# Latent attention: the 64 key columns of a pair's two heads as one 128-wide stationary, and all heads' values from one chunk of 512 columns

## The chip, the cores and the metric

The kernel runs on one core of a Trainium2 chip. The metric is the device time of one execution in microseconds (us). TensorE is called PE here, VectorE DVE, ScalarE ACT, and SyncE SP. ACT and DVE copy and transform what PE leaves in PSUM, and SP issues nearly all weight transfers.

## The reference, cut to what matters

The program is four transformer layers on 512 tokens of width 1024, all in float32. The change touches the first layer alone, in its latent attention with 8 heads:

```python
c_q, c_kv, k_r = proj[..., :o1], proj[..., o1:o2], proj[..., o2:o3]      # 256, 128, 32 columns
qA = (_rmsnorm(c_q, g_q) @ w_uq).reshape(B_, S, MLA_HEADS, MLA_QK)       # 8 heads x 96
kv = (_rmsnorm(c_kv, g_kv) @ w_ukv).reshape(B_, S, MLA_HEADS, MLA_NOPE + MLA_V)   # 8 x (64 + 64)
k_nope, vA = kv[..., :MLA_NOPE], kv[..., MLA_NOPE:]
oA = _mla_causal_attention(concat(q_nope, q_rope), concat(k_nope, k_rope), vA)
```

So from the 128-wide latent of each token come 64 key columns and 64 value columns for each of the 8 heads. The 32 rotated key columns are the same for all heads. After causal softmax attention, the outputs of this and of a second, dilated attention (8 heads) go through one output projection, and a feed-forward block and three further layers follow.

## The kernel before

**Matmuls in three parts.** Every projection is done in fp32r with both operands split in a rounded high part and a low remainder. `mm3` (lines 316 to 321) issues three matmuls for each tile product: high by high (L319), and the two mixed ones (L320, L321). Tokens lie along the free axis, 512 of them, so that most matmuls are 128x128 stationary by 128x512 moving.

**The weight ring.** Weights come in chunks, in one order that is fixed for the whole program (`ORDER`). Chunk c lives in slot c mod 3. Each chunk is loaded by a DMA of SP, rounded by ACT (`round_weights`, L337) and split by DVE (`split_weights`, L345); only then may PE use it (semaphore `w_split`). The low part overwrites the raw data, so the DMA of chunk c + 3 waits until PE has used chunk c (`w_used`). Where ACT and DVE prepare a chunk is written out by hand: `round_weights(act, upto)` and `split_weights(dve, upto)` prepare everything not yet prepared up to chunk `upto`.

**The attention steps.** Heads are worked in pairs: four latent pairs (`mla`, p = 0 to 3), then four dilated pairs (`dil`). `att_pe`, `att_act` and `att_dve` each run one `step` for each pair m. In step m, PE computes the scores of pair m (`scores`, 8 blocks, in float32), the projections of pair m + 1 in `pieces`, placed between the other work by a tuple of shares, the transposes of the probabilities of pair m - 1 (`turn`, 20 transposes in four groups) and their product with the values (`pv`). ACT does the exponentials of pair m (`exps`), the copies of the transposes of pair m - 1 (`copies`), and the staging of the projected keys and values of pair m + 1 (`keys`, `values`). DVE rotates the queries (`rotate`), scales and masks the scores (`masks`) and divides by the row sums (`norm`).

**The latent pieces before.** A latent pair has two chunks: 512 elements per partition for the queries (`w_e_uq`) and 256 for keys and values (`w_e_ukv`), the latter in the order of the reference: key columns of head 0, value columns of head 0, key columns of head 1, value columns of head 1. `keys` uses each head's 128 columns (64 of keys, 64 of values) as one stationary and stores from each result only the upper 64 rows, so it takes two tiles of three matmuls with 512 columns. `values` takes the value columns as the moving operand: for each of four token tiles, three matmuls with 128 columns. `queries` takes two tiles of six matmuls. In step 0 there is no pair before, so there are no transposes.

**Preparing chunks before.** In step m, ACT rounds up to `early(pairs, R, m)` after its first four exponentials, and up to the last chunk of pair m + 2 at the end of the step. DVE does the same between its masks and `norm`, and after `norm`. `early` is the last chunk of pair m + 2, less one where that pair is latent: in step 0 that is the chunk with the queries of pair 2.

Of the kernel before, what the change touches and what calls it, by code (L numbers as in the profile page):

```python
# [123 lines left out]
def _build(nc, dram, ctx):  # L124
# [14 lines left out]
    st_mla = stage(mixed, 4, [(W["w_e_uq"], 512, 0, 1), (W["w_e_ukv"], 256, 0, 1)])  # L139
# [50 lines left out]
    def area(name, specs, start):  # L190

        at, out = start, []
        for n, shape, dt in specs:
# [17 lines left out]
    (e_cqh, e_cql, e_ckh, e_ckl, e_q0, e_q1, e_k0, e_k1, e_v0, e_v1, e_p, e_t0, e_causal, e_ropeq), _ = area("mla", [  # L211
# [4 lines left out]
         ("v0", (P, TB, P), F32), ("v1", (P, TB, P), F32),  # L216
# [719 lines left out]

    def heads_v(A, p, j):

        if A.kind == "dil":
            return A.v[:, p, j * P:(j + 1) * P]  # L940
        return A.v[p % len(A.v)][:, j, :]
# [27 lines left out]
    def last_chunk(pairs, R, m):  # L969

        if m >= len(pairs):
            return R.st.base + m - len(pairs)
        A, p = pairs[m]
        return A.st.base + (2 * p + 1 if A.kind == "mla" else p)
# [8 lines left out]
    def att_pe(pe, pairs, ready, R):  # L983
# [10 lines left out]
        def pieces(A, p):  # L994
# [15 lines left out]
            if A.kind == "dil":  # L1010
                c = A.st.base + p

                def one(which, k):
                    w_h, w_l = chunk_w(c, KD, 256)
                    if k == 0:
                        if which == 0:
                            pe.wait_ge(w_split, c + 1)
                            if p == 0:
                                wait_for(pe, a_mla.s["v_staged"], 4)
# [6 lines left out]
            c = A.st.base + 2 * p  # L1026
# [10 lines left out]
            def keys():  # L1037
                w_h, w_l = chunk_w(c + 1, 1, 256)
                pe.wait_ge(w_split, c + 2)
                for hh in range(2):  # L1040
                    wait_for(pe, s["q_staged"], 2 * p + hh + 1)
                    tile(A0 + hh, w_h, w_l, hh * P, (e_ckh, e_ckl), range(1), 1)\
                        .then_inc(keys_made, 1)

            def values(half):
                w_h, w_l = chunk_w(c + 1, 1, 256)
                vh = w_h[:, 0, :].rearrange("p (a b) -> p a b", a=2)[:, :, 64:P]
                vl = w_l[:, 0, :].rearrange("p (a b) -> p a b", a=2)[:, :, 64:P]
                if half == 0:
                    wait_for(pe, s["k_staged"], 2 * p + 1)  # L1050
                for t in (2 * half, 2 * half + 1):
                    last = mm3(pe, ps[:, A0, t * P:(t + 1) * P], e_ckh[:, 0, t * P:(t + 1) * P],
                               e_ckl[:, 0, t * P:(t + 1) * P], vh, vl, True, True)
                if half == 1:
                    last.then_inc(w_used, 1)
# [47 lines left out]
        def pv(A, p):  # L1103
# [4 lines left out]
            if A.kind == "mla":  # L1108
                wait_for(pe, s["v_staged"], p + 1)
# [75 lines left out]
    keys_made = sem("mla_keys_made")  # L1185

    def early(pairs, R, m):

        return last_chunk(pairs, R, m + 2) - (1 if m + 2 < len(pairs) and pairs[m + 2][0].kind == "mla" else 0)

    def att_act(act, pairs, R):
        def load_table(A, p):
# [3 lines left out]
            if A.kind == "dil" and p == 0:  # L1196
                act.wait_ge(w_used, st_mla.base + 8)
# [11 lines left out]
        def values(A, p):  # L1209
            act.wait_ge(w_used, A.st.base + 2 * p + 2)  # L1210
            act.activation(A.v[p % 3][:, :, :], ps[:, A0, :].rearrange("p (a b) -> p a b", a=TB),
                           ACT.Copy).then_inc(A.s["v_staged"].sem, 1)
# [39 lines left out]
        def step(m, cur, nx, prev, pp):  # L1252
            mla_next = nx and nx[0].kind == "mla"
            if nx:
# [1447 lines left out]
```

## Time and profile before

| | us |
|---|---|
| median of the 3 timed runs | 2314.56 |
| timed runs | 2314.78, 2309.9, 2314.56 |
| the profiled execution, its time | 2311.96 |
| its span | 2310.2 |
| mean granted clock | 0.998 |

The span goes from the first to the last instruction; 1.8 us of the profiled execution lie outside it. All times of instructions below are counted from the span's start. PE is the engine with the most busy time, 2285.1 us. Its matmuls are pipelined: a row's duration holds the time until the result is out, and the next matmul starts before that, so that the distance between two starts tells the pace. The four latent steps run from 61.05 us to 122 us or so; they are under 3% of the span.

### The profile page before, as it was taken

The page shows a single profiled execution, that of the slowest core. Times are in us where ns is not written, and L with a number is a line of the kernel's source. Part 1 is how long each engine was busy: PE and PEld are TensorE (multiplying, and loading weights), DVE is VectorE, ACT ScalarE, POOL GpSimd, SP SyncE. Part 2 cuts the span into 40 slices and gives each one's busy share as a digit, 9 for nine tenths or more (in the row PEclk, how much of TensorE's full clock was granted, in tenths as well). Part 3 has the DMA queues.
Part 4 walks back from the last instruction along what each step waited for, and adds up shares of the span by engine and source line. Part 5 has one row for each costly group of instructions (what it writes and reads, how often), then busy time and mean ns, then how long its engine had stood idle before and what let it go on. Part 6 is the DMA issues. An engine that isn't in the chain of part 4 may idle for free.

```text
span 2310.2 us, 26274 instructions
## 1 busy us (share of the span) xinstructions
PE 2285.1 (99%) x10812; PEld 1856.3 (80%) x10812; DVE 1124.0 (49%) x1732; ACT 891.3 (39%) x1414; POOL 0.2 (0%) x4
## 2 busy tenths in 40 slices
PE   9999999999999999999999999999999999999999
PEld 7777888888778888888888788888886667888887
DVE  5655443344575443445677654334444675432432
ACT  5654322223474322224434443223344785321321
POOL 0000000000000000000000000000000000000000
PEclk9999999999999999999999999999999999999999
DMA  4222222322222223222221132322332112223222
GB/s 143 80 83 73 91 89 101 104 93 88 92 92 73 93 91 105 104 80 99 100 65 55 55 110 91 109 92 91 104 104 73 55 55 73 92 91 108 93 91 92
DMA packets 36583, 206.52 MB, mean 89 GB/s; under 512 B 4192, under 2 KB 5088, under 8 KB 17136
## 3 DMA queue, kind: packets, MB, share of 16 engines
q1 hardware_dynamic: 34128, 199.43, 25.3%
q10 hardware_dynamic: 2336, 5.41, 0.7%
q8 instruction: 86, 1.41, 0.2%
q14 instruction: 33, 0.27, 0.0%
HBM read 202.73 MB, written 2.10 MB: 89 GB/s over the span
## 4 chain that ended last, share of the span: by engine, by line
PE 96%; DVE 2%; ACT 1%; issue 1%; DVEq 0%; ACTq 0%
PE ps L319 29%; PE ps L321 29%; PE ps L320 29%; PE ps L1075 2%; PE ps L1684 1%; PE ps L1130 1%; PE ps L2042 1%; PE ps L2061 1%; PE ps L1099 1%; PE ps L1125 1%; PE ps L2052 1%; PE ps L1091 0%; DVE low_w L345 0%; PE ps L1709 0%; PE ps L583 0%
## 5 line engine op out<-in xcount | busy, mean ns | idle before, releaser
L319 PE MATMUL ps<-xh,high_w 128*128 128x512 f32 x1592 | 631.8, 397 | 0.0
L321 PE MATMUL ps<-xh,low_w 128*128 128x512 f32 x1592 | 620.5, 390 | 0.0
L320 PE MATMUL ps<-xl,high_w 128*128 128x512 f32 x1592 | 620.0, 389 | 0.0
L345 DVE TENSOR_TENSOR low_w<-raw_w,high_w 128x2048 fp32r<-128x2048 f32 (+3 forms) x208 | 422.9, 2034 | 174.2 <-ACT high_w L337 173.8
L337 ACT ACTIVATE high_w<-raw_w 128x2048 fp32r<-128x2048 f32 (+3 forms) x208 | 353.3, 1700 | 287.9 <-PE ps L321 281.4
L319 PEld LDWEIGHTS ps<-xh,high_w 128*128 128x128 f32 x1592 | 299.0, 188 | 65.1 <-issue 5.5
L321 PEld LDWEIGHTS ps<-xh,low_w 128*128 128x128 f32 x1592 | 298.8, 188 | 62.9
L320 PEld LDWEIGHTS ps<-xl,high_w 128*128 128x128 f32 x1592 | 299.2, 188 | 61.1 <-issue 1.4
L319 PE MATMUL ps<-ffn_hidh,high_w 128*128 128x512 f32 x864 | 336.1, 389 | 0.0
L320 PE MATMUL ps<-ffn_hidl,high_w 128*128 128x512 f32 x864 | 336.1, 389 | 0.0
L321 PE MATMUL ps<-ffn_hidh,low_w 128*128 128x512 f32 x864 | 336.1, 389 | 0.0
L713 DVE TENSOR_TENSOR h<-h,ps 128x512 f32<-128x512 f32 (+1 forms) x80 | 63.6, 794 | 327.7 <-PE ps L321 327.7
L320 PEld LDWEIGHTS ps<-ffn_hidl,high_w 128*128 128x128 f32 x864 | 162.2, 188 | 33.8
L319 PEld LDWEIGHTS ps<-ffn_hidh,high_w 128*128 128x128 f32 x864 | 162.2, 188 | 33.6
L321 PEld LDWEIGHTS ps<-ffn_hidh,low_w 128*128 128x128 f32 x864 | 162.2, 188 | 33.5
L761 ACT ACTIVATE squares_sq<-squares_sq 128x512 f32<-128x512 f32 x44 | 27.8, 632 | 334.7 <-DVE squares_sq L785 334.7
L785 DVE TENSOR_TENSOR squares_sq<-ps,rstd 128x512 f32<-128x512 f32 x44 | 30.4, 692 | 216.9 <-PE ps L321 205.9
L769 ACT ACTIVATE squares_sq<-squares_sq 128x512 f32<-128x512 f32 x64 | 39.3, 632 | 208.6 <-DVE squares_sq L801 208.6
L485 ACT ACTIVATE xh<-h,gains 128x512 fp32r<-128x512 f32 x56 | 38.7, 719 | 181.4 <-DVE h L713 178.6
L801 DVE SCALAR_TENSOR_TENSOR squares_sq<-ps,rstd 128x512 f32<-128x512 f32 x64 | 41.2, 686 | 126.4 <-PE ps L321 115.4
L319 PE MATMUL ps<-mix_oh,high_w 128*128 128x512 f32 x192 | 78.4, 408 | 0.0
L319 PE MATMUL ps<-high_w,xh 128*128 128x256 f32 (+1 forms) x224 | 76.7, 342 | 0.3 <-DVE low_w L345 0.3
(280 smaller groups left out, 2452.3 us busy)
## 6 DMA issues: line engine op xcount, KB each, us to landing
raw_w<-in_w_f_gu SPq DMA_DIRECT2D x44, 1024.0 KB, 4.9
raw_w<-in_w_m_up SPq DMA_DIRECT2D x32, 1024.0 KB, 4.8
raw_w<-in_w_m_dn SPq DMA_DIRECT2D x32, 1024.0 KB, 4.9
raw_w<-in_w_f_dn SPq DMA_DIRECT2D x32, 704.0 KB, 4.0
raw_w<-in_w_b_qk SPq DMA_DIRECT2D x8, 1024.0 KB, 4.9
raw_w<-in_w_e_qk SPq DMA_DIRECT2D x4, 1024.0 KB, 5.2
raw_w<-in_w_e_out SPq DMA_DIRECT2D x4, 1024.0 KB, 5.6
raw_w<-in_w_o_q SPq DMA_DIRECT2D x8, 512.0 KB, 3.6
```

The lines of the kernel that those rows point to most:

```text
L319: pe.matmul(out, sh, mh, start=start, stop=False)
L320: pe.matmul(out, sh, ml, start=False, stop=False)
L321: return pe.matmul(out, sl, mh, start=False, stop=stop)
L337: act.activation(wh[slot][:, 0:elems], raw[slot][:, 0:elems], ACT.Copy).then_inc(w_rounded, 1)
L345: dve.tensor_tensor(wl[slot][:, 0:elems], raw[slot][:, 0:elems], wh[slot][:, 0:elems].bitcast(F32), ALU.subtract).then_inc(w_split, 1)
L485: act.activation(hi[:, t, :], h[:, t, :], ACT.Copy, scale=weight(t)).then_inc(F.s["rounded"].sem, 1)
L713: dve.tensor_tensor(to, to, ps[:, 2 * par:2 * par + R.nt, :], ALU.add).then_inc(R.added.sem, 1)
L761: act.activation(sq[:, par, :], sq[:, par, :], ACT.Silu).then_inc(s["acted"].sem, 1)
L769: act.activation(sq[:, 2 + j, :], sq[:, j, :], ACT.Square).then_inc(s["acted"].sem, 1)
L785: dve.tensor_tensor(sq[:, par, :], ps[:, 2 * par, :], rstd[:, :], ALU.mult)\
L801: dve.scalar_tensor_tensor(out=sq[:, j, :], in0=ps[:, 2 * par + j, :], scalar=0.0, in1=rstd[:, :], op0=ALU.max, op1=ALU.mult)\
L1075: pe.matmul(score_block(A, n), heads_q(A, st, hh, i), heads_k(A, st, hh, i), start=True, stop=True).then_inc(s["scored"].sem, 1)
```

## The change

The weights for keys and values are packed in another way. Each pair now has a chunk `w_e_uk` of 128 elements per partition with the 64 key columns of both heads side by side, and one chunk `w_e_uv` of 512 elements holds the value columns of all eight heads. The latent stage has nine chunks instead of eight: queries 0, keys 0, queries 1, keys 1, all values, queries 2, keys 2, queries 3, keys 3. `keys` is one tile of three matmuls for a pair, and ACT takes its upper 64 rows for one head and its lower 64 rows for the other. `values(t)` is done once, in step 0, for one token tile t of 128 tokens and all heads: three matmuls with 512 columns, into four PSUM banks, which ACT copies one at a time into `e_v` and `xf`. `pv` of every latent pair reads from there.

```diff
-    st_mla = stage(mixed, 4, [(W["w_e_uq"], 512, 0, 1), (W["w_e_ukv"], 256, 0, 1)])
+    st_mla = stage(Stage, [entry for p in range(4) for entry in
+                           [(W["w_e_uq"], 512, p), (W["w_e_uk"], P, p)] + [(W["w_e_uv"], 512, 0)] * (p == 1)])
...
+    def mla_chunk(p):
+
+        return st_mla.base + 2 * p + (1 if p > 1 else 0)
+
+    st_mla_v = st_mla.base + 4
+    MLA_V_BANK = (O_BANK, T_BANK, T_BANK + 1, A1)
...
-                wait_past(pe, s["v_staged"], p)
+                if p == 2:
+                    wait_for(pe, s["v_staged"], 4)
...
             def keys():
-                w_h, w_l = chunk_w(c + 1, 1, 256)
+                w_h, w_l = chunk_w(c + 1, 1, P)
                 pe.wait_ge(w_split, c + 2)
-                for hh in range(2):
-                    wait_for(pe, s["q_staged"], 2 * p + hh + 1)
-                    tile(A0 + hh, w_h, w_l, hh * P, (e_ckh, e_ckl), range(1), 1)\
-                        .then_inc(keys_made, 1)
-
-            def values(half):
...
-            return [queries, keys, lambda: values(0), lambda: values(1)], (1, 1, 1, 0, 1)
+                wait_for(pe, s["q_staged"], 2 * p + 1)
+                tile(A0, w_h, w_l, 0, (e_ckh, e_ckl), range(1), 1).then_inc(w_used, 1)
+
+            def values(t):
+                w_h, w_l = chunk_w(st_mla_v, 1, 512)
+                if t == 0:
+                    pe.wait_ge(w_split, st_mla_v + 1)
...
+                last = mm3(pe, ps[:, MLA_V_BANK[t], :], e_ckh[:, 0, t * P:(t + 1) * P],
+                           e_ckl[:, 0, t * P:(t + 1) * P], w_h[:, 0, :], w_l[:, 0, :], True, True)
+                last.then_inc(w_used if t == 3 else latent_values_made, 1)
+            if p == 1:
+                return [queries, keys] + [lambda t=t: values(t) for t in range(TB)], (1, 2, 1, 1, 1)
+            return [queries, keys], (1, 1, 0, 0, 0)
...
+                if A.kind == "mla" and p == 1:
+                    wait_for(pe, s["v_staged"], 2)
+            if A.kind == "mla" and p == 1 and ns[0] == 4:
+                wait_for(pe, s["v_staged"], 3)
...
     def early(pairs, R, m):
 
+        if m == 0 and pairs[0][0].kind == "mla":
+            return st_mla_v
...
         def keys(A, p):
+            act.wait_ge(w_used, mla_chunk(p) + 2)
             for hh in range(2):
-                act.wait_ge(keys_made, 2 * p + hh + 1)
-                act.activation(A.k[p % 2][0:64, hh, :], ps[0:64, A0 + hh, :], ACT.Copy)\
+                act.activation(A.k[p % 2][0:64, hh, :], ps[64 * hh:64 * hh + 64, A0, :], ACT.Copy)\
...
             if mla_next:
                 keys(*nx)
+            if first_mla:
+                values(cur[0], (0,))
...
             exps(*cur, range(6, 7))
+            if first_mla:
+                values(cur[0], (1,))
...
-            if mla_next:
-                values(*nx)
+            if first_mla:
+                values(cur[0], (2, 3))
...
+            if m == 0 and cur[0].kind == "mla":
+                split_weights(dve, st_mla_v)
             if cur[0].kind != "swa":
                 masks(*cur, range(4, 8))
```

How this moves instructions is read from the instruction order of the two programs. On DVE, at the end of step 0 before the change (low_w_59 is the low part of the queries' chunk of pair 2, low_w_57 that of its keys and values, the RECIPROCAL and the eight TENSOR_SCALAR after it are `norm`; the rows with squares_sq begin step 1):

```order
L1336 ISA small 128x1
L345 TENSOR_TENSOR low_w_59<-raw_w_56,high_w_53 128x512
L1352 RECIPROCAL small<-small 128x8
L1356 TENSOR_SCALAR mla_p<-mla_p,small 128x128
L1356 TENSOR_SCALAR mla_p<-mla_p,small 128x256
L1356 TENSOR_SCALAR mla_p<-mla_p,small 128x384
...
L345 TENSOR_TENSOR low_w_57<-raw_w_54,high_w_51 128x256
L1336 ISA squares_sq,small<-ps,mla_causal 128x128
```

And the same place on DVE with the change (low_w_57 is now the low part of the queries' chunk of pair 2, low_w_58 that of its keys):

```order
L1364 ISA small 128x1
L1380 RECIPROCAL small<-small 128x8
L1384 TENSOR_SCALAR mla_p<-mla_p,small 128x128
L1384 TENSOR_SCALAR mla_p<-mla_p,small 128x256
L1384 TENSOR_SCALAR mla_p<-mla_p,small 128x384
...
L346 TENSOR_TENSOR low_w_57<-raw_w_54,high_w_51 128x512
L346 TENSOR_TENSOR low_w_58<-raw_w_55,high_w_52 128x128
L1364 ISA squares_sq,small<-ps,mla_causal 128x128
```

The split of the chunk with the queries of pair 2 has moved from ahead of `norm` to behind it. In its old place ahead of the masks, not shown, stands the split of the chunk with all values.

On ACT, in step 0 before the change, from the fifth exponential on (L1220 with mla_p is an exponential, L1206 stages keys, L1211 values, L337 rounds a chunk):

```order
L337 ACTIVATE high_w_53<-raw_w_56 128x512
L1220 ACTIVATE mla_p,small<-mla_p,small 128x384 x2
L1206 ACTIVATE mla_k_70<-ps 64x512 x2
L1220 ACTIVATE mla_p,small<-mla_p,small 128x512 x2
L1211 ACTIVATE mla_v_72<-ps 128x512
L337 ACTIVATE high_w_51<-raw_w_54 128x256
```

And the same stretch of ACT with the change (L1244 is an exponential, L1226 stages keys, L1235 values, L338 rounds a chunk):

```order
L338 ACTIVATE high_w_53<-raw_w_56 128x512
L1244 ACTIVATE mla_p,small<-mla_p,small 128x384 x2
L1226 ACTIVATE mla_k_70<-ps 64x512 x2
L1235 ACTIVATE mla_v<-ps 128x512
L1244 ACTIVATE mla_p,small<-mla_p,small 128x512
L1235 ACTIVATE mla_v<-ps 128x512
L1244 ACTIVATE mla_p,small<-mla_p,small 128x512
L1235 ACTIVATE xf<-ps 128x512 x2
L338 ACTIVATE high_w_51<-raw_w_54 128x512
L338 ACTIVATE high_w_52<-raw_w_55 128x128
```

Two copies of values now stand ahead of the last exponential. The rounding of the queries' chunk of pair 2, once the first row of this stretch, now stands behind the four copies.

## Rows read from the trace of the kernel before

**Rows 1.** The page: span and busy time of PE.

```profile
span 2310.2 us, 26274 instructions
PE 2285.1 (99%) x10812; PEld 1856.3 (80%) x10812; DVE 1124.0 (49%) x1732; ACT 891.3 (39%) x1414; POOL 0.2 (0%) x4
```

**Rows 2.** Instructions of the tile mla_ckh: durations min/median/max, first and last start.

```profile
L319 PE MATMUL ps<-high_w,mla_ckh x16: 222/274/327, 59.8 to 100.4; 128*128 128x128 f32 x16
```

**Rows 3.** Timeline 58.2 to 62.3 us: start, duration, engine, line, [idle before <-releaser].

```profile
58.25 0.39 PE L320 MATMUL ps<-mla_ckl,high_w 128*128 128x512 f32 x1
58.47 0.39 PE L321 MATMUL ps<-mla_ckh,low_w 128*128 128x512 f32 x1
58.90 0.59 ACT L1206 ACTIVATE mla_k<-ps 64x512 f32<-64x512 f32 x1 [0.97 <-PE ps L321]
...
59.76 0.22 PE L319 MATMUL ps<-high_w,mla_ckh 128*128 128x128 f32 x1
...
60.46 0.92 ACT L337 ACTIVATE high_w<-raw_w 128x512 fp32r<-128x512 f32 x2
...
61.05 1.52 PE L1075 MATMUL ps<-mla_k,mla_q 128*128 128x128 f32 x8
61.11 1.03 DVE L345 TENSOR_TENSOR low_w<-raw_w,high_w 128x512 fp32r<-128x512 f32 x2 [2.20 <-ACT high_w L337]
...
62.23 0.58 PE L319 MATMUL ps<-mla_cqh,high_w 128*128 128x512 f32 x1
```

**Rows 4.** Timeline 65.3 to 74.4 us, the rest of step 0 and after.

```profile
65.36 0.69 DVE L1307 TENSOR_TENSOR mla_q<-ps,mla_ropeq 128x512 f32<-128x512 f32 x1 [0.67 <-PE ps L321]
...
68.48 0.69 DVE L1336 CUSTOM_DVE_ANT_0 mla_p<-ps,mla_causal 128x512 f32<-128x512 f32 x1 [0.16 <-PE ps L1075]
...
69.06 1.27 ACT L1206 ACTIVATE mla_k<-ps 64x512 f32<-64x512 f32 x2 [0.99 <-PE ps L321]
...
70.94 0.71 ACT L1220 ACTIVATE mla_p<-mla_p,small 128x512 f32<-128x512 f32 x1
...
71.10 1.52 PE L1075 MATMUL ps<-mla_k,mla_q 128*128 128x128 f32 x8
...
71.64 0.58 ACT L1211 ACTIVATE mla_v<-ps 128x512 f32<-128x512 f32 x1
71.77 0.20 DVE L1352 RECIPROCAL small<-small 128x8 f32<-128x8 f32 x1 [1.99 <-ACT mla_p L1220]
...
72.32 0.54 PE L319 MATMUL ps<-mla_cqh,high_w 128*128 128x512 f32 x1
...
74.38 0.42 DVE L345 TENSOR_TENSOR low_w<-raw_w,high_w 128x256 fp32r<-128x256 f32 x1
```

**Rows 5.** Timeline of step 1: first transposes, staging of keys, first pv matmul.

```profile
78.20 0.49 PE L1099 MATMUL ps<-ident,mla_p 128*128 128x128 f32 x3
...
80.21 1.06 ACT L1206 ACTIVATE mla_k<-ps 64x512 f32<-64x512 f32 x2
...
84.87 0.64 PE L1130 MATMUL ps<-mla_t,mla_v 128*64 128x512 f32 x1 [0.16 <-ACT mlat_t L1243]
```

**Rows 6.** Windows: ACT in step 1; columns are us, ACT busy, PEclk, DMA.

```profile
78.51:84.87 6.36, 6.36 (x19) 1.00 0.01 3
```

**Rows 7.** Waits of PE over the whole span: total, times, longest.

```profile
PE ps L1684 <- DVE gla_ks L1865: 4.3, 4, 1.8
PE ps L2052 <- DVE small L2296: 2.5, 1, 2.5
PE ps L2022 <- ACT squares_sq L2133: 2.4, 1, 2.4
```

**Rows 8.** Windows of PE just after those three longest waits.

```profile
1299.80:1303.90 4.10, 3.95 (x14) 0.59 0.00 0
1779.60:1783.00 3.40, 3.40 (x13) 1.00 0.53 222
1908.10:1911.50 3.40, 3.40 (x13) 0.50 0.00 0
```

More of the change, by code:

```diff
@@ L973, in last_chunk @@
         A, p = pairs[m]
-        return A.st.base + (2 * p + 1 if A.kind == "mla" else p)
+        return mla_chunk(p) + 1 if A.kind == "mla" else A.st.base + p
     def att_steps(pairs, step, tail):
@@ L1024, in pieces @@
                 return [lambda a=a, k=k: one(a, k) for a in range(2) for k in range(KD)], (4, 3, 3, 3, 3)
-            c = A.st.base + 2 * p
+            c = mla_chunk(p)
             def queries():
@@ L1037, in keys @@
             def keys():
-                w_h, w_l = chunk_w(c + 1, 1, 256)
+                w_h, w_l = chunk_w(c + 1, 1, P)
                 pe.wait_ge(w_split, c + 2)
-                for hh in range(2):
-                    wait_for(pe, s["q_staged"], 2 * p + hh + 1)
-                    tile(A0 + hh, w_h, w_l, hh * P, (e_ckh, e_ckl), range(1), 1)\
-                        .then_inc(keys_made, 1)
-            def values(half):
[L1046 to L1055, printed above, removed]
-            return [queries, keys, lambda: values(0), lambda: values(1)], (1, 1, 1, 0, 1)
+                wait_for(pe, s["q_staged"], 2 * p + 1)
[4 more added lines that the diff above has]
+                    pe.wait_ge(w_split, st_mla_v + 1)
+                elif t == 3:
+                    wait_for(pe, s["q_staged"], 4)
+                else:
+                    wait_for(pe, s["masked"], 3 + t)
+                last = mm3(pe, ps[:, MLA_V_BANK[t], :], e_ckh[:, 0, t * P:(t + 1) * P],
[4 more added lines that the diff above has]
+            return [queries, keys], (1, 1, 0, 0, 0)
         def scores(A, p, ns):
@@ L1108, in pv @@
             if A.kind == "mla":
-                wait_for(pe, s["v_staged"], p + 1)
+                wait_for(pe, s["v_staged"], 4)
             if A.kind == "swa" and p == 0:
@@ L1196, in load_table @@
             if A.kind == "dil" and p == 0:
-                act.wait_ge(w_used, st_mla.base + 8)
+                act.wait_ge(w_used, st_mla.base + 9)
             wait_past(act, A.s["masked"], 8 * (p - 1))
@@ L1203, in keys, with values @@
         def keys(A, p):
+            act.wait_ge(w_used, mla_chunk(p) + 2)
             for hh in range(2):
-                act.wait_ge(keys_made, 2 * p + hh + 1)
-                act.activation(A.k[p % 2][0:64, hh, :], ps[0:64, A0 + hh, :], ACT.Copy)\
+                act.activation(A.k[p % 2][0:64, hh, :], ps[64 * hh:64 * hh + 64, A0, :], ACT.Copy)\
                    .then_inc(A.s["k_staged"].sem, 1)
[L1209 to L1212, printed above, removed]
+        def values(A, ts):
+            for t in ts:
+                if t == 3:
+                    act.wait_ge(w_used, st_mla_v + 1)
+                else:
+                    act.wait_ge(latent_values_made, t + 1)
+                act.activation(latent_values(t), ps[:, MLA_V_BANK[t], :], ACT.Copy)\
+                   .then_inc(A.s["v_staged"].sem, 1)
         def exps(A, p, ns):
@@ L1253, in step @@
             mla_next = nx and nx[0].kind == "mla"
+            first_mla = m == 0 and cur[0].kind == "mla"
             if nx:
@@ L1292, in att_act @@
             round_weights(act, last_chunk(pairs, R, 1))
-            values(*pairs[0])
         att_steps(pairs, step, tail)
@@ L1303, in rotate @@
                 if hh:
-                    dve.wait_ge(w_used, A.st.base + 2 * p + 1)
+                    dve.wait_ge(w_used, mla_chunk(p) + 1)
                 else:
@@ L2621, in lay_out @@
     arrays["w_e_uq"] = panels(a["e_w_uq"][0], [np.concatenate(cols[2 * i:2 * i + 2]) for i in range(4)])
-    arrays["w_e_ukv"] = panels(a["e_w_ukv"][0], [r(256 * i, 256 * i + 256) for i in range(4)])
+    heads = r(1024).reshape(8, 2, 64)
+    arrays["w_e_uk"] = panels(a["e_w_ukv"][0], [heads[2 * i:2 * i + 2, 0].reshape(-1) for i in range(4)])
+    arrays["w_e_uv"] = panels(a["e_w_ukv"][0], [heads[:, 1].reshape(-1)])
     q0, k0, v0 = 416, 416 + 512, 416 + 1024
```

14 lines of the change are left out of this document (9 added, 5 removed).

## The prediction

> **What bounds the kernel now.** I read the page first. PE is busy for 2285.1 of 2310.2 us [rows 1], so work that is taken from PE is gained where nothing else ends last, and only there. The change touches less than 3% of the span, the latent steps, so I then read their timeline.
>
> The reader is to see three stretches there. In the *opening* (58 to 61 us), PE goes from the key tiles through the value matmuls to the scores. The matmuls with 512 columns start 0.22 to 0.23 us apart [rows 3]. I take 0.227. The twelve with 128 columns take from 59.76 to 61.05, 0.108 each [rows 3], where a quarter of the columns would be 0.057.
>
> In *step 0* there is no other pair to turn, and PE runs nearly without a wait to the scores of step 1 at 71.10 and the queries of pair 2 at 72.32 [rows 4]. DVE does `norm` just then: the reciprocal at 71.77, the next split at 74.38 [rows 4]. The queries of pair 2 didn't have to wait for it, because their chunk was split ahead of `norm`.
>
> In *step 1* (and step 2 repeats it) the engine that sets the end is another one. The first transposes start at 78.20, `pv` at 84.87 after a wait for ACT's last copy [rows 5], and from 78.51 to 84.87 ACT is busy for 6.36 of 6.36 us [rows 6]: copies, two exponentials, the staging of keys, copies, and so on, each in the order written. PE's keys, transposes and value matmuls lie inside this stretch and are not what it waits for.
>
> **The change part by part.** *Counted on PE alone.* Keys lose 4 x 3 = 12 matmuls of 512 columns, 12 x 0.227 = 2.7 us. The 48 value matmuls of 128 columns (16 on each of three lines [rows 2], 4 x 1.3 = 5.2 us) become 12 of 512. The trace doesn't show these with this stationary; the bounds are 12 x 0.108 = 1.3, if the added columns were free, and 12 x 0.39 = 4.7, if none overlapped the next [rows 3]. I take 12 x 0.227 = 2.7 us, the pace of the rows with as many columns. So values gain 2.5 us. By count the change is worth 5.2 us. The Trainium skill ("TensorE: Matmul & The Clock Gate", section on the back-to-back issue gap) gives about 81 ns for a matmul with 128 columns and 131 ns for one with 512 in a stream that reloads weights; by it keys would give 12 x 0.131 = 1.6 and values 3.9 - 1.6 = 2.3, together 3.9 us. The rows above don't agree with either figure, and they decide.
>
> *The opening.* The keys' only tile starts when the first of two did and its last matmul is the one at 58.47; ACT took its result at 58.90 [rows 3]. Now ACT copies both heads from it. Two such copies in a row take 1.06 us where one takes 0.59 [rows 3, 5], so a row ends with about 0.1 that the next instruction overlaps, and ACT is free after 0.96. So the scores can start at 58.90 + 1.06 + 0.06 = 60.02 instead of 61.05 [rows 3]. Of 2.0 us of PE work removed here (0.7 keys, 1.3 values) 1.03 is gained, the rest becomes a wait of PE for ACT. The rounding of the next chunk moves from 60.46 to 59.86, its split from 61.11 to 60.5, done by 61.2 [rows 3]; the queries of pair 1 start at 61.25, not 62.23. From here step 0 runs 0.97 ahead.
>
> That the second copy reads PSUM partitions 64 to 127 and writes 0 to 63 is shown nowhere. Below it costs what the other one does, 0.59 [rows 3]; above I put twice that, 0.6 more in each step. I take nothing.
>
> *Step 0.* The second rotation starts at 64.39 instead of 65.36 and takes 0.69 [rows 4]. Behind it now stands the split of the values' chunk, 0.69 for 512 elements like this, and pushes the four masks back by up to 0.6, so the last one starts no later than its 68.48 of before [rows 4], while ACT stages keys: that is cover enough. PE finishes the keys 0.97 + 0.69 earlier than before; ACT took the first tile at 69.06 and takes the only tile at 68.09. Then ACT's order decides: keys 0.96, values(0) 0.58, an exponential 0.71, values(1) 0.58, and the last exponential starts at 70.9, as before at 70.94 [rows 4]. All that was gained is gone on ACT by now. PE's twelve value matmuls end their issue at 70.6 (72.6 by the upper bound, still ahead of the stall below); the scores of step 1 wait for values(1) and start at 70.95, 0.15 ahead of before.
>
> *Where it stalls.* Behind the last exponential ACT does values(2), values(3) (1.2) and rounds the queries' chunk of pair 2 (0.62), until 73.4. DVE had split that chunk ahead of `norm`. Now `norm` comes first. It begins at 71.73, 0.83 behind the last exponential's start as before (70.94 to 71.77), and takes 2.61 (71.77 to 74.38) [rows 4], until 74.35. Then the split takes 0.69, until 75.05. PE, in order, stands at the queries of pair 2: ready at 72.15, held to 75.05. Before, they began at 72.32 with a first matmul that took 0.15 more than usual, so 72.4. **Loss: 2.65 us.** PE's queue behind it holds the scores 4 to 7 and the transposes, and ACT's chain of step 1 starts with the transposes.
>
> The wait for `v_staged` 4 in `queries` (ACT at 72.7) and the other new waits end before that. The DMAs are no later: each of the nine chunks is issued when its slot is free, all of it before the stall, and the large chunks behind them come one slot earlier than before.
>
> *Steps 1 and 2.* PE loses 0.7 of keys and 1.3 of values in each, 4.0 us, inside the stretch of 6.67 us from the first transposes to `pv` [rows 5], all of it ACT's [rows 6]. ACT's list in that stretch is the same with the change (its copy of values came behind it). Gain: nothing. Without this cover it would be 4.0. Step 3 and all behind it stream on PE and keep the shift.
>
> *The clock.* The three longest waits of PE in the span are 1.8, 2.5 and 2.4 us [rows 7]. After the first, the granted clock is 0.59 over 4.1 us; after the second, 0.50 over 3.4 us, the lower of the two levels; after the third it stays at 1.00 [rows 8]. The new wait is about 2.5 us without any matmul in flight. At half clock for 3.4 us with PE's work on the path the loss is at most 1.7; I take 1.6. The chance is 2 in 3 by count; I take 6 in 10, since there are only three cases. The Trainium skill ("TensorE: Matmul & The Clock Gate", section on the clock gate) says that the lower level is the default and activity releases it, which these rows bear out.
>
> *The sum.* 2.65 + 1.6 = 4.25. Against the profiled execution's own 2311.96 (span 2310.2 and 1.8 around it) this gives 2316.2; against the median of the three runs, 2314.56, which is 2.6 higher, 2318.8. The four executions scatter over 4.9 us, so I take the middle of the two bases, 2313.3, and predict **2317.5 us**, 0.18% more than before. What a measurement of this kernel can tell from no change is 0.2%, 4.6 us.
>
> **The rivals.**
>
> *The stall alone.* The clock stays. For it speaks the wait of 2.4 us after which it did [rows 8]. 2313.3 + 2.65 = 2316.0.
>
> *PE is the bound in steps 1 and 2 after all.* The page says 99% PE [rows 1], and if ACT had slack of its own that is only filled because PE delays it, the 4.0 us would come back. Against it: ACT's 6.36 of 6.36 us. 2313.3 + 2.65 - 4.0 = 2311.9.
>
> *The other side: no stall.* If `norm` and the split before PE's queries took no longer than to 72.4, the count would hold: 2313.3 - 5.2 = 2308.1. It decides at the point where the split ends by 72.4, and the order puts 2.6 us of `norm` ahead of it that can't start before the last exponential. Only if PE waited elsewhere anyway would it not show.
>
> *A dearer one, slower by more than 0.2%.* The staging of head 1's keys across partitions costs 0.6 more each time: once in the opening, once in step 0 ahead of the last exponential, once each in the chains of steps 1 and 2. In the opening and in step 0 it moves the same stall, so it counts once there; 3 x 0.6 = 1.8 on top of 4.25: 2313.3 + 6.0 = 2319.3. With 0.13 more for each it crosses the bound of 4.6. Against it: a copy of 64 partitions takes 0.59 and one of 128 partitions 0.58 [rows 3, 4], so partitions don't matter for its time.
>
> **How the numbers follow.** Stall with the fall of the clock 0.42, stall alone 0.28, dearer 0.12, PE the bound 0.10, no stall 0.08. The range leaves out no stall and the upper half of the dearest: 2311.5 (PE the bound, less 0.4) to 2320.5 (dearest with the higher base). Faster by over 0.2% is no stall, 0.08. Slower by over 0.2% is the dearer case and, since 4.25 lies just under 4.6, somewhat under half of the first, 0.12 + 0.19 = 0.31. The rest, 0.61, is within 0.2%.
>
> **What would show it right or wrong.** After: the first matmul with mla_cqh of pair 2 starts about 2.9 us behind the scores of step 1, and its releaser is DVE's low_w, behind the eight TENSOR_SCALAR. ACT's last exponential of step 0 stands behind a copy of values and starts at 70.7 to 71.1. From the first transposes of step 1 to its `pv` 6.7 us pass as before, with PE less busy. From the scores of step 1 to those of step 2 it takes 2.8 us longer, or 4.4 with a PEclk of 0.5 in it; from there to the end the shift is constant. It would be wrong if ACT's stretch in steps 1 and 2 got shorter, if PE's wait in front of the queries ended at 73 us, or if the shift at step 3's start were not the shift at the end.

## The result and the profile after

The changed kernel takes 2321.13 us (median of 5 runs, 2317.91 to 2322.5), the kernel before 2313.95 us (median of 5, 2309.9 to 2314.78). The ratio is 1.0034, with a 95% interval of 1.0023 to 1.0045: slower by 7.2 us by the medians and by 7.9 us by the ratio, where 2317.5 and a difference of 4.25 were forecast. The time lies outside the range of 2311.5 to 2320.5.

The profiled execution took 2321.05 us. Its page, where the kernel before had 2285.1 us of PE in 2310.2 [rows 1]:

```profile
span 2319.3 us, 26183 instructions
PE 2283.9 (98%) x10764; PEld 1852.1 (80%) x10764; DVE 1124.6 (48%) x1733; ACT 891.7 (38%) x1415; POOL 0.2 (0%) x4
```

PE has 48 matmuls less and is busy for 1.2 us less, and the span is 9.1 us longer. The opening and step 0 on the timeline, which answers to [rows 3] and [rows 4] (start, duration, engine, line, [idle before <-releaser]; L1226 stages keys, L1235 values, L1244 is an exponential, L1384 is the last part of `norm`, L346 a split):

```profile
58.82 1.21 ACT L1226 ACTIVATE mla_k<-ps 64x512 f32<-64x512 f32 x2 [0.98 <-PE ps L322]
60.13 1.55 PE L1093 MATMUL ps<-mla_k,mla_q 128*128 128x128 f32 x8 [1.34 <-issue]
...
71.08 0.72 ACT L1244 ACTIVATE mla_p<-mla_p,small 128x512 f32<-128x512 f32 x1
...
71.44 1.55 PE L1093 MATMUL ps<-mla_k,mla_q 128*128 128x128 f32 x8 [0.59 <-ACT mla_v L1235]
...
71.92 0.20 DVE L1380 RECIPROCAL small<-small 128x8 f32<-128x8 f32 x1 [3.64 <-ACT mla_p L1244]
72.16 2.46 DVE L1384 TENSOR_SCALAR mla_p<-mla_p,small 128x128 f32<-128x128 f32 x8
...
74.53 0.89 DVE L346 TENSOR_TENSOR low_w<-raw_w,high_w 128x512 fp32r<-128x512 f32 x2
75.27 0.50 PE L320 MATMUL ps<-mla_cqh,high_w 128*128 128x512 f32 x1 [2.28 <-DVE low_w L346]
```

The scores of step 0 start at 60.13 instead of 61.05, after 1.34 us of idle time for which the row names no releaser; they start 0.10 behind the end of the two key copies (58.82 + 1.21). The last exponential starts at 71.08, `norm` makes way for the next split at 74.53, and the queries of pair 2 start at 75.27 behind DVE's split, after a wait of 2.28 us. Steps 1 and 2, which answer to [rows 5]:

```profile
81.14 0.49 PE L1117 MATMUL ps<-ident,mla_p 128*128 128x128 f32 x3
...
83.15 1.20 ACT L1226 ACTIVATE mla_k<-ps 64x512 f32<-64x512 f32 x2
84.37 0.98 ACT L1267 ACTIVATE mla_t<-ps 128x384 f32<-128x384 f32 x2
85.00 0.30 PE L1117 MATMUL ps<-ident,mla_p 128*128 128x128 f32 x1 [1.91 <-ACT mla_t L1267]
...
88.11 1.11 PE L1148 MATMUL ps<-mla_t,mla_v 128*64 128x512 f32 x1 [0.69 <-ACT mlat_t L1267]
...
92.57 2.20 PE L1093 MATMUL ps<-mla_k,mla_q 128*128 128x128 f32 x8
...
94.42 0.58 PE L320 MATMUL ps<-mla_cqh,high_w 128*128 128x512 f32 x1
...
104.24 0.30 PE L1117 MATMUL ps<-ident,mlap_p 128*128 128x128 f32 x1 [1.91 <-ACT mla_t L1267]
...
107.35 0.95 PE L1148 MATMUL ps<-mla_t,mla_v 128*64 128x512 f32 x1 [0.80 <-ACT mlat_t L1267]
...
111.34 1.58 PE L1093 MATMUL ps<-mla_k,mla_q 128*128 128x128 f32 x8
```

And PE in three windows of the same execution (us, PE busy, PEclk, DMA): its queries right behind the wait of 2.28 us, then the two stretches in which the granted clock was low.

```profile
75.27:78.14 2.87, 2.87 (x12) 1.00 0.00 0
87.07:93.89 6.82, 6.13 (x24) 0.50 0.01 2
107.55:110.96 3.41, 3.41 (x12) 0.50 0.47 154
```

The reader is to see that the first transposes come 2.94 us later than before (81.14 for 78.20 [rows 5]), and that this is not the end of it. A `pv` matmul with 512 columns, which took 0.64 [rows 5], takes 1.11. The clock did not fall behind the wait of 2.28 us, where it stayed at 1.00. It fell to 0.50, its level of 1.2 GHz, late in step 1 for 6.8 us and again late in step 2 for 3.4 us. What PE waited for between 60 and 116 us (total, times, longest):

```profile
PE ps L1117 <- ACT mla_t L1267: 4.2, 4, 1.9
PE ps L320 <- DVE low_w L346: 2.3, 1, 2.3
PE ps L1148 <- ACT mlat_t L1267: 1.5, 2, 0.8
PE ps L1093 <- issue: 1.3, 1, 1.3
PE ps L1117 <- ACT mlat_t L1267: 0.9, 2, 0.5
PE ps L1093 <- ACT mla_v L1235: 0.6, 1, 0.6
```

Together 10.8 us. The same view of the kernel before, in the same stretch, adds up to 1.6 us: its second key tile and half of its value matmuls stood in the place of the wait of 1.9 us of each step, the other half ahead of `pv`.

### The profile page after: what moved, and what is told of

Its sections match the earlier page's. It is cut to its first block, busy times and chain, and to the rows that moved or that the text cites. A ratio compares the mean times of both kernels' runs of the same rounds, so it can differ in the third digit from the quotient of the medians.

```text
span 2319.3 us, 26183 instructions
## 1 busy us (share of the span) xinstructions
PE 2283.9 (98%) x10764; PEld 1852.1 (80%) x10764; DVE 1124.6 (48%) x1733; ACT 891.7 (38%) x1415; POOL 0.2 (0%) x4
## 4 chain that ended last, share of the span: by engine, by line
PE 95%; DVE 2%; ACT 2%; issue 1%; ACTq 0%; DVEq 0%
PE ps L320 29%; PE ps L322 28%; PE ps L321 28%; PE ps L1093 2%; PE ps L1714 1%; PE ps L1148 1%; PE ps L2072 1%; PE ps L2091 1%; PE ps L1117 1%; PE ps L1143 1%; PE ps L2082 1%; PE ps L1109 0%; DVE low_w L346 0%; PE ps L1739 0%; PE ps L584 0%
## 5 line engine op out<-in xcount | busy, mean ns | idle before, releaser
L346 DVE TENSOR_TENSOR low_w<-raw_w,high_w 128x2048 fp32r<-128x2048 f32 (+4 forms) x209 | 423.0, 2026 | 173.4 <-ACT high_w L338 173.0
L338 ACT ACTIVATE high_w<-raw_w 128x2048 fp32r<-128x2048 f32 (+4 forms) x209 | 353.4, 1693 | 288.2 <-PE ps L322 281.5
```

The source lines that it names most:

```text
L338: act.activation(wh[slot][:, 0:elems], raw[slot][:, 0:elems], ACT.Copy).then_inc(w_rounded, 1)
L346: dve.tensor_tensor(wl[slot][:, 0:elems], raw[slot][:, 0:elems], wh[slot][:, 0:elems].bitcast(F32), ALU.subtract).then_inc(w_split, 1)
```

## The experiments

The experiments were timed in three groups of four, each in turns with the kernel before; the changed kernel's row is the result above. The first group is fill, early, keysonly and novals; the second is fill_a1, early_fill_a1, keys_a1 and keys_dve; the third, on another chip than these two, is fill_all, early_fill_all, early_dve and before_dve. The ratio is to the kernel before in the same group. "Clock" is the mean, over the timed runs, of the granted TensorE clock that each run lists. "Step 3" is when its scores start in the profiled execution, in us, a stretch that ends ahead of everything the kernels have in common. One execution of `early` took 8171.46 us and is left out, so its ratio rests on four.

Two things limit what the table can tell. The profiled execution is one of the timed ones and often an extreme one: in fill_all and early_dve it is the fastest of 11, in novals, early_fill_all, keys_dve and before_dve the slowest of 11. And the mean clock also holds the falls behind step 3, where the code is the same. In the profiled executions the lower clock there adds up to 10.2 us in the kernel before and in the changed one, but to 13.6 in novals, 17.0 in keys_dve, 20.4 in early_fill_all and 23.8 in before_dve, which has no fall at all between 60 and 116 us. A difference of 0.001 in the mean clock of some ten executions therefore doesn't say by itself where the clock fell.

Three accounts of the loss stand against each other in the expectations. Clock theory: the removed matmuls kept PE busy beside ACT's list, and without them the clock falls. Stall theory: the late split and the dearer key copies are all of it. PE-bound theory: PE's work is what ends these steps, so less of it is faster.

| kernel | ratio (95% interval) | clock | step 3 |
|---|---|---|---|
| before | 1 | 0.9980, 0.9981, 0.9975 in the three groups | 103.3 |
| changed | 1.0034 (1.0023 to 1.0045) | 0.9956 | 111.3 |
| early | 1.0038 (1.0025 to 1.0052) | 0.9942 | 109.6 |
| fill | 1.0030 (1.0018 to 1.0041) | 0.9963 | 107.3 |
| fill_a1 | 1.0025 (1.0016 to 1.0033) | 0.9967 | 110.1 |
| fill_all | 1.0016 (1.0007 to 1.0025) | 0.9969 | 106.7 |
| early_fill_a1 | 1.0019 (1.0010 to 1.0028) | 0.9963 | 110.1 |
| early_fill_all | 1.0012 (1.0003 to 1.0021) | 0.9969 | 105.3 |
| novals | 1.0013 (1.0004 to 1.0022) | 0.9965 | 106.5 |
| keysonly | 1.0032 (1.0022 to 1.0042) | 0.9952 | 110.6 |
| keys_a1 | 1.0025 (1.0015 to 1.0035) | 0.9949 | 107.1 |
| keys_dve | 0.9987 (0.9978 to 0.9995) | 0.9979 | 101.6 |
| before_dve | 1.0008 (0.9999 to 1.0017) | 0.9969 | 105.7 |
| early_dve | 1.0006 (0.9997 to 1.0015) | 0.9963 | 103.8 |

**Less work alone (novals).** The edit of the kernel before leaves out 22 of the 24 small value matmuls of pairs 2 and 3, so that their values are not computed, and adds no wait:

```diff
+                if p > 1:
+                    if half == 1:
+                        pe.matmul(ps[:, A0, 3 * P:TOK], e_ckh[:, 0, 3 * P:TOK], vh, start=True, stop=True)\
+                            .then_inc(w_used, 1)
+                    return
```

> The kernel before, which leaves out 11 of the 12 value matmuls of each of pairs 2 and 3 (the values of these pairs are wrong; ACT still copies the bank). 22 matmuls, 2.4 us of PE work less, nothing added, no wait added. Clock theory: PE now waits about 1.7 us in each of steps 1 and 2 and the clock falls behind it, so the kernel with less work gets slower by 2 to 4.5 us, 1.0009 to 1.0020, PEclk 0.5 for 3.4 to 6.8 us between 80 and 112 us. Stall theory: no change, 1.0000. PE-bound theory: 2.4 us faster, 0.9990.

It is slower by 0.13%, 3.0 us, as the clock theory had forecast (1.0009 to 1.0020). PE in step 1, where the matmuls are gone, and the window that follows:

```profile
81.99 0.30 PE L1104 MATMUL ps<-ident,mla_p 128*128 128x128 f32 x1 [0.93 <-ACT mla_t L1248]
...
85.08 1.11 PE L1135 MATMUL ps<-mla_t,mla_v 128*64 128x512 f32 x1 [0.72 <-ACT mlat_t L1248]
...
84.30:91.10 6.80, 6.08 (x23) 0.50 0.45 157
```

Waits of 0.93 and 0.72 us stand where the value matmuls were, none as long as those that the prediction looked at. The clock falls at 84.31, behind the first of them and two of 0.18 and 0.46 us, and stays at 0.50 for 6.8 us; the wait of 0.72 lies in the fall. From the first transposes to `pv` it takes 6.67 us (78.41 to 85.08), as before: the work taken away was worth nothing. Step 2 then starts at 89.5 for 87.17 of before and step 3 at 106.5 for 103.3, 3.1 us later, of which 0.2 was there ahead of step 1. This execution is the slowest of the 11 and lost as much again behind step 3. The timed runs say the same another way: at a mean clock of 0.996 novals averages 2317.4 us (7 executions) and the kernel before 2317.0 (3 in the same group), so what separates them is how often the clock is low. Shown: idle time of PE in ACT's stretch costs by the clock, without any other part of the change.

**The work put back (fill, fill_a1, fill_all).** The changed kernel, with matmuls whose results nobody reads. fill and fill_a1 put back the 12 small value matmuls of each of pairs 2 and 3, fill_all the second key tile too. This is fill_all's edit. fill_a1 lacks the first three lines and waits for the second query tile instead of the first key copy; fill writes to the keys' bank `A0` and waits for both key copies:

```diff
+                if p > 1:
+                    wait_for(pe, s["q_staged"], 2 * p + 2)
+                    tile(A1, w_h, w_l, 0, (e_ckh, e_ckl), range(1), 1)
...
+            def filler(half):
+                w_h, w_l = chunk_w(c + 1, 1, P)
+                if half == 0:
+                    wait_for(pe, s["k_staged"], 2 * p + 1)
+                for t in (2 * half, 2 * half + 1):
+                    last = mm3(pe, ps[:, A1, t * P:(t + 1) * P], e_ckh[:, 0, t * P:(t + 1) * P],
+                               e_ckl[:, 0, t * P:(t + 1) * P], w_h[:, 0, :], w_l[:, 0, :], True, True)
...
+            if p > 1:
+                return [queries, keys, lambda: filler(0), lambda: filler(1)], (1, 1, 1, 0, 1)
```

> The changed kernel, and for pairs 2 and 3 PE again does the 12 value matmuls of 128 columns of each pair where they stood before, with the keys' chunk as moving operand; nobody reads the result. Clock theory (PE's value matmuls kept PE busy beside ACT's chain, and without them the granted clock falls): with more work the kernel gets faster by about 4.5 us against the changed one, PEclk 1.00 from 80 to 112 us, step 2 starts 2.7 us earlier and step 3 4.4 us earlier than in the changed kernel; ratio to the kernel before about 1.0015. Stall theory (the wait for the low part of pair 2's queries and the dearer key copies are all of it): no change against the changed kernel, ratio 1.0034. PE-bound theory: up to 2.6 us slower than the changed kernel, 1.0045.

> As fill, but the unread value matmuls go to the bank of the second query tile and so need not wait for the key copies, which left a wait of 1.3 us in fill. Clock theory: no wait of PE over 1 us and no PEclk under 1.00 between 80 and 115 us in most executions; mean granted clock of the timed runs 0.997 to 0.998 (changed kernel 0.995 to 0.996); ratio to before 1.0014 to 1.0020, what is left being the wait of 2.3 us at 75 us, 0.7 for the start of step 1 and 0.25 to 0.3 for the key copies in each of steps 1 and 2. Stall theory: 1.0034 as the changed kernel.

> The changed kernel, with all of PE's work of before back in steps 1 and 2 and unread: for pairs 2 and 3 a second key tile of three matmuls with 512 columns and the 12 value matmuls, in the bank of the second query tile, the values behind the first key copy as before. fill and fill_a1 left out the key tile and kept waits of 1.3 us. Clock theory: mean granted clock of the timed runs back at 0.998 (changed kernel 0.9956), ratio 1.0012 to 1.0018, which is the stall of step 1 (2.9 us) and the dearer key copies (0.3 in each of steps 1 and 2) alone. If PE's waits in steps 1 and 2 are not what brings the clock down: mean clock stays at 0.996, ratio 1.0025 to 1.0034.

fill_all has all of PE's work of before in steps 1 and 2, and more work makes it faster than the changed kernel. Its PE from 80 to 112 us, and its waits in front of the transposes there:

```profile
80.00:112.00 32.00, 29.70 (x163) 1.00 0.34 116
PE ps L1132 <- ACT mla_t L1286: 1.1, 4, 0.3
PE ps L1132 <- ACT mlat_t L1286: 0.9, 2, 0.5
```

The clock is 1.00 throughout, no wait is over 0.5 us, the longest of the kernel before there, and step 3 starts at 106.7 instead of 111.3, with the wait of 2.3 us at 75 us still there. The ratio is 1.0016, as was forecast for the stall and the copies alone. The mean clock was forecast to come back to 0.998; it is 0.9969, against 0.9975 of its group. The interval (1.0007 to 1.0025) only just overlaps that of the changed kernel (1.0023 to 1.0045), and the two were not timed in the same group, so the gain in the timed runs is likely rather than beyond doubt. At equal mean clock fill_all is 2.3 to 3.1 us slower than the kernel before of its group, and the changed kernel 2.2 to 3.0, so what separates these two is the clock.

fill and fill_a1 lie above the forecast of the clock theory (1.0015, and 1.0014 to 1.0020) with 1.0030 and 1.0025. Waits of 1.3 us remained in their steps 1 and 2. In fill's profiled execution the clock held all the same, in fill_a1's it fell at 102.7 us for 6.8 us. Each ratio is within the other's interval and within that of the changed kernel. fill's interval (1.0018 to 1.0041) leaves out the 1.0015 but not the 1.0034 of the stall theory, and fill_a1's (1.0016 to 1.0033) reaches from the forecast to just short of 1.0034. So the timed runs leave open whether the half fills give anything.

**The stall alone taken away (early).** ACT rounds the queries' chunk of pair 2 ahead of values(0), DVE splits it ahead of `norm`:

```diff
+                round_weights(act, st_mla_v + 1)
                 values(cur[0], (0,))
...
+            if m == 0 and cur[0].kind == "mla":
+                split_weights(dve, st_mla_v + 1)
```

> The changed kernel, with the queries' chunk of pair 2 rounded by ACT ahead of values(0) and split by DVE ahead of norm. Stall theory: the wait of 2.3 us at 75.3 is gone, transposes of step 1 start 2.3 to 2.9 us earlier, ratio to the kernel before about 1.0022 to 1.0024. Clock theory: the same 2.3 to 2.9 us come back, but the waits of 1.9 us in steps 1 and 2 and the fall of the clock behind them remain, 4.5 us of them, so the kernel stays slower than before, 1.0022; if the wait at 75.3 was what made the clock fall at 87, the clock now stays and the ratio is about 1.0010.

The wait at 75.3 is gone, and the first transposes of step 1 start at 79.5 instead of 81.14. That is less than expected, since ACT's list of step 0 is now longer by the rounding and the scores of step 1 start at 72.1. The clock falls at 85.1 us for 6.8 us and at 105.6 for 3.4 us as in the changed kernel, without a wait over 2 us anywhere near. Step 3 starts 1.7 us earlier. By the timed runs nothing is gained: the ratio is 1.0038 where both theories had about 1.0022, it overlaps the changed kernel's almost wholly, and the mean clock, of four executions, is the lowest of all. So the wait for the split is not what brings the clock down.

**Both (early_fill_a1, early_fill_all).** Their edits are those above together.

> fill_a1 and early together. If the late split and the missing fill are all of the loss beside the key copies: ratio 1.0005 to 1.0012 (early had the transposes of step 1 at 79.5, 1.3 us behind the kernel before, and each key staging costs 0.3). If the fall of the clock has another cause than PE's waits in steps 1 and 2: 1.0025 or more.

> fill_all and early together: the queries' chunk of pair 2 is prepared ahead of norm too. Clock theory: mean clock 0.998, ratio 1.0004 to 1.0010. Otherwise 1.0019 or more, as early_fill_a1.

early_fill_all is at 1.0012, a little above the 1.0004 to 1.0010 expected, with step 3 at 105.3 and no fall of the clock between 60 and 116 us in its profile. What remains of 2.0 us there is the start of step 1, 1.1 us late since PE waits for ACT's copies of the values of all pairs, 0.2 more up to the first transposes, and 0.3 in each chain for the keys. early_fill_a1, with waits of 1.3 us left, had the lower clock for 3.4 us from 85.9 and for 6.8 us from 103.0 in its profile. Its 1.0019 lies between the two forecasts, 1.0005 to 1.0012 and 1.0025 or more, and decides nothing.

**The keys' part alone (keysonly, keys_a1, keys_dve).** The kernel before with the chunk packed as both heads' keys, then both heads' values, and one key tile:

```diff
-                for hh in range(2):
-                    wait_for(pe, s["q_staged"], 2 * p + hh + 1)
-                    tile(A0 + hh, w_h, w_l, hh * P, (e_ckh, e_ckl), range(1), 1)\
+                wait_for(pe, s["q_staged"], 2 * p + 1)
+                tile(A0, w_h, w_l, 0, (e_ckh, e_ckl), range(1), 1).then_inc(keys_made, 1)
```

In keysonly the values use the same bank as the keys, and wait for both copies. In keys_a1 they use the bank of the second query tile. keys_dve is keys_a1 with the second head's copy on DVE:

```diff
+        def second_keys(A, p):
+            dve.wait_ge(keys_made, p + 1)
+            dve.tensor_copy(A.k[p % 2][0:64, 1, :], ps[64:P, A0, :]).then_inc(A.s["k_staged"].sem, 1)
...
             split_weights(dve, early(pairs, R, m))
+            if nx_kind == "mla":
+                second_keys(*nx)
```

> The kernel before with the keys' part of the change alone: the pair's chunk holds both heads' key columns, then both heads' value columns, one key tile for a pair, values for each pair as before. Clock theory: the value matmuls still fill PE beside ACT's chain; only the second key copy costs 0.25 us more in steps 1 and 2, the opening gains some tenths (PE waits for both copies before the values), ratio 0.9998 to 1.0006. PE-count theory: 12 matmuls of 0.227 less, 2.7 us faster, 0.9988. If the keys' part alone lets the clock fall, 1.0015 or more, with PEclk under 1.00 between 80 and 112 us.

> As keysonly, but the values go to the bank of the second query tile, so that they need not wait for both key copies (keysonly had a wait of 1.3 us in front of the values of every pair). Clock theory: the waits and the fall of the clock at 61, 85 and 106 us are gone; ratio 0.9995 to 1.0006, mean clock 0.998. If one key tile for two heads is dear by itself, 1.003 as keysonly.

> As keys_a1, and DVE takes the second head's key copy, behind its masks, where it waits for ACT anyway. ACT's stretch from the first transposes to pv gets shorter by one key copy, 0.5 to 0.6 us in steps 1 and 2 each, the opening by about 0.7 us: ratio 0.9985 to 0.9995 if the clock holds. If ACT's order isn't what ends steps 1 and 2: as keys_a1. A shorter stretch leaves PE less to wait for, so the clock should hold better than in keys_a1.

The first two miss the forecast of the clock theory (0.9998 to 1.0006, 0.9995 to 1.0006) and come out at the dear end that was named beside it. I had overlooked that one tile for both heads makes the values wait for two copies where they waited for one: four waits of 1.3 us in keysonly, and the clock falls at 61, 85 and 106 us. In keys_a1, with fewer matmuls and the longer copies, waits of 1.3 us stand in front of the third group of transposes, and the clock falls at 99.9 us. Both have 12 large matmuls less than before and are slower.

keys_dve is faster than the kernel before, and than the changed one. Its waits of PE on ACT in the same stretch, and the copy on DVE beside ACT's:

```profile
PE ps L1096 <- ACT mla_t L1238: 1.4, 4, 0.5
PE ps L1096 <- ACT mlat_t L1238: 0.9, 2, 0.5
...
79.09 0.69 DVE L1307 COPY mla_k<-ps 64x512 f32<-64x512 f32 x1
...
79.46 0.58 ACT L1202 ACTIVATE mla_k<-ps 64x512 f32<-64x512 f32 x1
```

From the first transposes to `pv` it takes 6.18 us (77.45 to 83.63) instead of the 6.67 of before, and step 3 starts 1.7 us earlier. No fall of the clock lies between 60 and 116 us. The profiled execution as a whole is the slowest of the 11, 2314.2 us, with 17.0 us at the lower clock behind step 3; the median is 2309.86.

**Where keys_dve's gain comes from (before_dve, early_dve).** The same copy on DVE in the kernel before with its two key tiles, and in `early`, that is in the whole change:

> The kernel before, with DVE taking the second head's key copy alone (two key tiles for a pair, old packing). It tells how much of keys_dve's 0.9987 is the key tile. If ACT's list is what ends steps 1 and 2, most of the gain is here: 0.9988 to 0.9996. If the one key tile is what pays: 1.0000.

> The whole change with the early preparation of the queries' chunk of pair 2 and with DVE taking the second head's key copy, no filler. ACT's stretch in steps 1 and 2 gets 0.6 us shorter each, ACT's list of step 0 too, so the stall at 72 to 75 us nearly goes: by the shifts alone 0.9985 to 0.9995. Clock theory: PE waits more than in keys_dve (no value matmuls in steps 1 and 2), the clock falls as in the changed kernel (mean 0.996) and gives back 3 to 5 us: 1.0000 to 1.0012, slower than keys_dve (0.9987). If only ACT's list counts: 0.9985 or less.

before_dve has the short chain in step 1 (80.57 to 86.76), but not in step 2, where it takes 7.16 us (96.24 to 103.40) and PE waits 1.21 us for DVE's copy. Its step 0 starts 1.6 us late: DVE's copy has to wait for the second key tile, and the values in the first bank wait for both copies, so step 1 starts at 73.5 for 71.1. It is not faster, 1.0008, where 0.9988 to 0.9996 or 1.0000 was expected. So the copy on DVE pays with one key tile and a bank of its own for the values, not by itself. early_dve has no small value matmuls and no filler; its step 2 starts at 86.8, 0.4 earlier than before. Then the clock falls at 99.5 us, and it ends at 1.0006 with a mean clock of 0.9963, against 0.9979 of keys_dve, which keeps the small value matmuls in steps 1 and 2.

## Why the prediction was wrong

**The opening** was right: scores from 60.13, forecast 60.02. The queries of pair 1 started at 61.33, forecast 61.25.

**Step 0 and the stall** were right: the last exponential at 71.08 (forecast 70.9), `norm` until 74.5 (74.35), queries of pair 2 from 75.27 (75.05). Only the scores of step 1 came later than forecast, 71.44 for 70.95, without effect on the stall. The shift at the first transposes is 2.94 us (2.65). That ACT's list gives back all that the opening gained, and that moving one split behind `norm` costs more than that, came out as read.

**The keys' staging across partitions**, taken at nothing with an upper bound of 0.6, costs 0.3: the pair takes 1.20 instead of 1.06 and the next instruction starts 1.22 behind instead of 0.96 (83.15 to 84.37; the kernel before had 80.21 [rows 5] and 81.17). Each copy by itself still takes 0.58 to 0.59; what is lost is the overlap of the second with its neighbours, which start 0.60 and 0.62 us apart instead of 0.48. From the first transposes to `pv` it is 6.97 instead of 6.67, twice, 0.6 us in all. The dearer rival's extra cost was real, at half its price.

**The failing step** is "Steps 1 and 2 ... Gain: nothing." Nothing was gained, as said, but the step priced the removed work at nothing, and it was worth something. PE's second key tile and value matmuls were not on ACT's path; they filled PE's time beside it. Without them PE waits 1.9 us in front of the third group of transposes in each of the two steps, and 0.7 to 0.8 ahead of `pv`. The clock fell to half at 87.07, just ahead of the wait for `pv`, and at 107.55, 0.2 us into `pv`, so PE did `pv` at the lower clock, and in step 1 the next scores too; both are on the path. From `pv` to the scores of the next step it took 4.46 us in step 1 and 3.99 in step 2, where `pv` had taken 2.30 each time (84.87 [rows 5] to 87.17, 101.03 to 103.33), and the four scores behind step 1 took 1.85 instead of 1.23: 2.16 + 0.62 + 1.69 = 4.5 us. With the stall's 2.94 and the copies' 0.6 this makes 8.0, the shift of step 3 (111.34 for 103.33).

**The term for the clock** had the right size for one fall of 3.4 us (1.6, measured 1.69 in step 2) and the wrong place and number: 1.6 in all, where the two falls cost 4.5. It was tied to the one wait that looked long, chosen by the three waits in [rows 7]. The clock did not fall behind it, fell twice elsewhere, and the experiments show it to go with the shorter, repeated waits: novals fell behind waits of 0.93, 0.18 and 0.46 us. The Trainium skill ("TensorE: Matmul & The Clock Gate", section on the clock gate) says that the clock is set by how busy PE has been recently. The traces agree in the main: in the 5.9 us from the first transposes to the fall at 84.31 PE is busy for 4.33 us in novals, and in the same stretch of the kernel before, which kept its clock, for 5.20. But fill's profiled execution kept it too, with 4.12 of 5.95 us (81.55 to 87.50), so PE's busy time there doesn't decide it alone. I had used the section on one wait and not on the two steps in which the change makes PE idle.

**The rest**, 1.1 us of the profiled executions' 9.1, lies behind step 3, in code that is the same. Most of it is where one fall of the clock lies. In the third layer two groups of PE's matmuls each wait for DVE, 5.3 us apart. First the kernel before, then the changed one:

```profile
1299.82 1.39 PE L1684 MATMUL ps<-gla_qs,gla_ks 128*128 128x128 f32 x8 [1.82 <-DVE gla_ks L1865]
1305.12 1.13 PE L1684 MATMUL ps<-gla_qs,gla_ks 128*128 128x128 f32 x8 [1.34 <-DVE gla_ks L1865]
1307.47 1.05 PE L1684 MATMUL ps<-gla_qs,gla_ks 128*128 128x128 f32 x8
...
1307.37 1.13 PE L1714 MATMUL ps<-gla_qs,gla_ks 128*128 128x128 f32 x8 [1.82 <-DVE gla_ks L1895]
1312.68 2.05 PE L1714 MATMUL ps<-gla_qs,gla_ks 128*128 128x128 f32 x8 [2.78 <-DVE gla_ks L1895]
1316.54 1.05 PE L1714 MATMUL ps<-gla_qs,gla_ks 128*128 128x128 f32 x8
```

In the kernel before the clock falls at 1300.5, between the two groups: PE's matmuls last longer, its wait is 1.34 us and not 2.78, and the second group still starts 5.30 us behind the first, so this fall costs nothing. In the changed kernel it falls at 1312.5, behind the wait, and the next group starts 3.86 us on instead of 2.35: 1.5 us. The shift was 7.55 us ahead of this place, 0.5 less than at step 3, and is 9.1 behind it. fill_all, early_dve and keysonly have the fall between the groups too (1303.2, 1301.0 and 1307.3 us). Why it falls in the one place or the other, no run tested.

The kernel before itself scatters by 8 us in 33 runs, and with its clock: its runs of 0.999 average 2311.3 us, those of 0.996 2317.5 in the same group. At 0.996 the changed kernel's average 2320.0, where the kernel before has 2317.0 to 2317.8 in the three groups. So some 2.2 to 3.0 us of the difference are not the clock's, where the trace has 3.5 for the stall and the copies; a step of 0.001 in the clock as listed is worth 2.3 us, and each average rests on two or three executions.

**The chances.** The likeliest case's mechanism was half right; the sum of 4.25 was just below what counts as slower, and 0.61 for no change rested on it. The rivals "PE is the bound" and "no stall" are refuted by novals (less work gained nothing) and by the timeline. The sign that the shift stays constant behind the scores of step 2 failed as well: it grew from 5.4 us there to 8.0 at step 3.

## What to carry to other kernels

On PE, where it waits for another engine's list, removing work is not free of charge just because the work was off the path: ask what stood beside the path and whether PE's clock is held up by it. Sum up its new waits over the whole stretch, not the longest one alone. When a preparation step is moved to make room, look at what it is now queued behind. And take the work off the engine whose list ends the stretch first: one copy from ACT to DVE, with one key tile and a bank of their own for the values, gave 0.9987, where the whole change with its 48 fewer matmuls and its stall had cost 0.34%.

## What the runs showed of the hardware that I had not expected

The clock falls without any long wait: in novals PE was busy for 2.6 of the 4.2 us from 80.1 to 84.3, its longest wait 0.93 us, and the clock was 0.50 for the next 6.8 us. It stayed at 1.00 behind a single wait of 2.28 us. Where it falls differs between kernels whose waits in steps 1 and 2 are as long (fill and fill_a1, 1.3 us in each), and between executions of one kernel the mean clock goes from 0.995 to 0.999, which is worth some 6 us. What a fall costs depends on what PE does in it: 1.7 us for 3.4 us at the lower clock with `pv` on the path, nothing where PE would have waited for DVE anyway. Two ACT copies of 64 partitions by 512 elements from PSUM, both to partitions 0 to 63, take 1.20 us when the second reads partitions 64 to 127 of the same bank, and 1.06 when both read 0 to 63, of two banks. No run tells the partitions from the bank.
